# A mixture-of-experts stage whose 64-slot passes run beside 128-slot passes, chunk by chunk

## What is computed

```python
D_MODEL, D_FF, N_EXPERTS, TOP_K = 1024, 2816, 8, 2

def swiglu(h, w1, w3, w2):
    return (jax.nn.silu(h @ w1) * (h @ w3)) @ w2

def moe_ffn(h, router, w1, w3, w2):
    ht = h.reshape(-1, shape[-1])
    logits = (ht @ router).astype(jnp.float32)
    top_v, top_i = lax.top_k(logits, TOP_K)
    wts = jax.nn.softmax(top_v, axis=-1)
    combine = jnp.sum(jax.nn.one_hot(top_i, N_EXPERTS, dtype=jnp.float32) * wts[..., None], axis=1)
    # for every expert: out += combine[:, e] * swiglu(ht, w1[e], w3[e], w2[e])
```

## Time and profile before

| | before |
|---|---|
| median of three runs | 1789.32 us |
| lowest and highest of them | 1788.54 and 1793.39 us |
| the profiled execution | 1784.65 us |
| its span, first to last instruction | 1782.8 us |
| TensorE busy | 1676.5 us (94%) |
| VectorE busy | 1021.3 us (57%) |
| ScalarE busy | 792.6 us (44%) |
| read from HBM | 404.73 MB |

### The profile page before, as it was taken

The page is one execution under the profiler, slowest core; times in us unless marked ns, Lnnn a source line. Parts: engine busy times, 40 slices in busy tenths (PEclk is TensorE's granted clock), DMA queues, the critical chain, the costliest instruction groups (busy, mean ns, idle before and its releaser), DMA issues.

```text
span 1782.8 us, 25642 instructions
## 1 busy us (share of the span) xinstructions
PE 1676.5 (94%) x10193; PEld 1294.4 (73%) x10193; DVE 1021.3 (57%) x1415; ACT 792.6 (44%) x1225; POOL 55.0 (3%) x40
## 2 busy tenths in 40 slices
PE   5999987999999999999977999999999999988896
PEld 3877656988888888797767887677788888544443
DVE  3326656677677533733676987657889897100012
ACT  4417544532212222734655766556677776100101
POOL 0000000000000000000000530000000000000000
PEclk9999968999999999999988999999999999999998
DMA  8411053154467532131013986668989998999998
GB/s 335 161 62 72 1 188 144 72 189 174 157 228 262 197 116 95 57 142 63 33 50 142 352 331 227 247 230 328 361 341 356 345 368 313 378 406 421 419 420 363
DMA packets 56831, 407.53 MB, mean 229 GB/s; under 512 B 6322, under 2 KB 6450, under 8 KB 7808
## 3 DMA queue, kind: packets, MB, share of 16 engines
q1 hardware_dynamic: 56128, 404.38, 59.2%
q0 software_dynamic: 288, 0.79, 0.1%
q10 hardware_dynamic: 288, 0.63, 0.1%
HBM read 404.73 MB, written 1.05 MB: 228 GB/s over the span
## 4 chain that ended last, share of the span: by engine, by line
PE 82%; DMA 7%; DVE 6%; ACT 4%; issue 1%; SPq 0%; POOL 0%; ACTq 0%; DVEq 0%
PE psum L2273 60%; DMA raw<-units 5%; PE psum L2887 4%; PE psum L2897 2%; PE psum L2783 2%; DMA raw_more<-units 2%; PE psum L2841 1%; PE psum L2913 1%; PE psum L2925 1%; PE psum L2290 1%; PE psum L2472 1%; PE psum L2299 1%; DVE w_lo L1572 1%; PE psum L2496 1%; ACT xn L1026 1%
## 5 line engine op out<-in xcount | busy, mean ns | idle before, releaser
L1572 DVE TENSOR_TENSOR w_lo<-raw,w_hi 128x1024 fp32r<-128x1024 f32 x130 | 153.0, 1219 | 143.9 <-ACT w_hi L990 143.5
L2273 PE MATMUL psum<-act_hi,w_hi 128*128 128x512 f32 (+1 forms) x608 | 220.3, 362 | 2.8 <-DVE w_lo L1572 2.8
L2273 PE MATMUL psum<-act_hi,w_lo 128*128 128x512 f32 (+1 forms) x608 | 218.1, 359 | 0.0
L2273 PE MATMUL psum<-act_lo,w_hi 128*128 128x512 f32 (+1 forms) x608 | 218.0, 359 | 0.0
L990 ACT ACTIVATE w_hi<-raw 128x1024 fp32r<-128x1024 f32 x130 | 130.4, 1053 | 164.2 <-DMA raw<-units 89.8
L2044 DVE TENSOR_TENSOR w_lo<-raw,w_hi 128x2048 fp32r<-128x2048 f32 x75 | 171.4, 2289 | 45.4 <-ACT w_hi L1378 45.1
L1378 ACT ACTIVATE w_hi<-raw 128x2048 fp32r<-128x2048 f32 x75 | 143.8, 1918 | 73.0 <-PE psum L2273 43.8
L2273 PE MATMUL psum<-w_hi,act_hi 128*128 128x256 f32 (+1 forms) x368 | 131.2, 357 | 4.3 <-DVE act_lo L1651 2.4
L2044 DVE TENSOR_TENSOR w_lo<-raw_more,w_hi 128x2048 fp32r<-128x2048 f32 x49 | 112.1, 2289 | 35.7 <-ACT w_hi L1378 35.4
L2273 PE MATMUL psum<-w_hi,xt_hi 128*128 128x512 f32 x332 | 132.2, 398 | 0.0
L2093 DVE TENSOR_TENSOR e_act<-e_sil,psum 128x256 f32<-128x256 f32 (+1 forms) x88 | 32.2, 366 | 172.6 <-ACT e_sil L1452 172.6
(11 more groups left out here) (364 smaller groups left out, 3210.5 us busy)
## 6 DMA issues: line engine op xcount, KB each, us to landing
raw<-units SPq DMA_DIRECT2D x275, 1024.0 KB, 5.1
raw_more<-units SPq DMA_DIRECT2D x107, 1024.0 KB, 6.8
...
```

Source lines behind the costliest of these rows:

```text
L1572: ins = dve.tensor_tensor(w_lo[:, w_slot(i), part], raw[:, i % RING, part], w_hi[:, w_slot(i), part].bitcast(F32), ALU.subtract)
L2273: ins = pe.matmul(dst, lhs(a), rhs(b), start=first and n == 0, stop=last and n == 2)
```

## The change

The narrow passes are now p3, p5 and p7 (`NARROW`), and the experts that they take are the same three least used (`PLACE_OF_RANK`). Passes p2 and p3, p4 and p5, p6 and p7 run as pairs: `run_steps` yields rows, and a row of a pair holds one chunk of the full pass and one of the narrow. In such a row TensorE's order is: the full chunk's up (two units), the narrow chunk's up (two units), the turns of the row before, full and narrow, then the downs of the row before that, full and narrow. Each row so has six units. PSUM banks and several SBUF buffers are assigned anew, so that both passes have their own.

`splits_at` takes the place of `split_behind`. In p0 and p1 the splits run four units ahead as before, but only within these passes; in paired rows a unit is split in its own row, with none ahead. ScalarE and VectorE split the full up units first, copy the turns of the row before behind them, then take the SiLU or product of the full chunk, the split of the full down unit, and the SiLU or product of the narrow chunk.

The outputs of both passes of a pair are brought to SBUF in chunk 2 of the next pair, and their eight scatters stand in its chunks 2 to 9. The gathers are spread over chunks 7 to 10 as single pieces; those of p3 move into the wide pass, beside p2's. `finish` scatters, and VectorE adds, the output of both last passes, eight pieces instead of four. To bring the experts into the new places VectorE writes eight constants (`place_wanted`) in p0, and treats the narrow places one by one in `ranked` and `next_task`, which runs three times.

```diff
+PLACE_OF_RANK = (0, 1, 2, 5, 3, 6, 4, 7)
...
-def run_steps(passes):
-
-    g0, g1 = passes[0] * FC, (passes[-1] + 1) * FC
-    for g in range(g0, g1 + 2):
-        yield g if g < g1 else None, g - 1 if g0 <= g - 1 < g1 else None, g - 2 if g0 <= g - 2 else None
+NARROW, SLOTS = (3, 5, 7), 64
+FIRST_PAIR = 2
+
+def is_narrow(p):
+
+    return p in NARROW
+
+def run_steps(r):
+
+    rows = []
+    for p in RUNS[r]:
+        if not is_narrow(p):
+            beside = (p + 1,) if is_narrow(p + 1) else ()
+            rows += [tuple(q * FC + c for q in (p,) + beside) for c in range(FC)]
+    for i in range(len(rows) + 2):
+        yield tuple(rows[j] if 0 <= j < len(rows) else () for j in (i, i - 1, i - 2))
+
...
+SINGLE_SPLITS = sum(m < UNIT_AT["up", FIRST_PAIR * FC, 0] for m in SPLIT_LIST)
...
-def split_behind(r, key):
-
-    s = SPLIT_OF[UNIT_AT[key]] + W_RING
-    return [s] if s < split_limit(r) and s != LATE_SPLIT else []
-
-
-LATE_SPLIT = SPLIT_OF[UNIT_AT["down", NARROW[0] * FC - 1]]
+    return split_end(r) + (W_RING - 1 if r else 0)
+
+def splits_at(r, key):
+
+    s = SPLIT_OF[UNIT_AT[key]]
+    if r == 0 and s >= SINGLE_SPLITS:
+        return [s]
+    return [s + W_RING] if s + W_RING < (split_limit(r) if r else SINGLE_SPLITS) else []
+
+def last_passes(r):
+
+    return tuple(p for p in RUNS[r] if p > RUNS[r][-1] - 1 - is_narrow(RUNS[r][-1]))
+
+def scatters_at(r, p, c):
+
+    if r or p == 0 or is_narrow(p):
+        return []
+    if p == WIDE:
+        return [(0, c - SCATTER_STEP)] if SCATTER_STEP <= c < SCATTER_STEP + 4 else []
+    first = SCATTER_STEP - 1
+    out = [(p - 2 if p > FIRST_PAIR else WIDE, c - first)] if first <= c < first + 4 else []
+    return out + ([(p - 1, c - first - 4)] if first + 4 <= c < first + 8 and p > FIRST_PAIR else [])
+
...
+def outputs_at(r, p, c):
+
+    if r or c != 2 or p == 0 or is_narrow(p):
+        return []
+    return [p - 1] if p <= FIRST_PAIR else [p - 2, p - 1]
+
+def is_paired(r, i):
+
+    return r == 0 and i >= FIRST_PAIR * FC
+
...
+def gather_pieces(r, p, c):
+
+    if r or p == 0 or is_narrow(p) or not 0 <= c - GATHER_STEP < 4:
+        return []
+    a = p + 1 if p == WIDE else p + 2
+    pieces = [[(a, 0)], [(a, 1)], [(a, 2), (a + 1, 0)], [(a + 1, 1), (a + 1, 2)]][c - GATHER_STEP]
+    return [piece for piece in pieces if piece[0] <= EXPERTS]
 
 
...
         def run(r):
-            for up, turned, down in run_steps(RUNS[r]):
-                p, c = divmod(up, FC) if up is not None else (None, None)
-                if up is not None:
+            for i, (ups, turned, downs) in enumerate(run_steps(r)):
+                full = [g for g in ups if not is_narrow(g // FC)]
+                for g in full:
+                    p, c = divmod(g, FC)
                     if p == WIDE + 1 and c == 2:
                         wide_output()
-                    if not is_narrow(p):
-                        for s in split_behind(r, ("up", up, 0)):
+                    for s in splits_at(r, ("up", g, 0)):
+                        high(s)
+                    if p < FIRST_PAIR:
+                        for q in outputs_at(r, p, c):
+                            output(q)
+                    if p == WIDE:
+                        silu(g)
+                        wide_silu(g)
+                    for s in splits_at(r, ("up", g, 1)):
+                        high(s)
+                if is_paired(r, i):
+                    for g in full:
+                        for q in outputs_at(r, *divmod(g, FC)):
+                            output(q)
+                    for g in turned_into_rows(r, i):
+                        columns_turned(g)
+                    for q, piece in gathered_into_rows(r, i):
+                        half_high(q, piece) if piece < 2 else selection_turned(q)
+                for g in full:
+                    if g // FC != WIDE:
+                        silu(g)
+                if is_paired(r, i):
+                    for g in downs[:1]:
+                        for s in splits_at(r, ("down", g)):
                             high(s)
-                    if c == 2 and 0 < p < EXPERTS:
-                        output(p - 1)
-                    if p == WIDE:
-                        silu(up)
-                        wide_silu(up)
-                    if not is_narrow(p):
-                        for s in split_behind(r, ("up", up, 1)):
-                            high(s)
-                    if p != WIDE:
-                        silu(up)
-                if turned is not None:
-                    columns_turned(turned)
-                if down is not None and not is_narrow(down // FC):
-                    for s in split_behind(r, ("down", down)):
+                    for g in ups[1:]:
+                        silu(g)
+                    continue
+                for g in turned_into_rows(r, i):
+                    columns_turned(g)
+                for g in downs[:1]:
+                    for s in splits_at(r, ("down", g)):
                         high(s)
-                if up == NARROW[0] * FC:
-                    high(LATE_SPLIT)
-                if p == WIDE and c in (GATHER_STEP, GATHER_STEP + 1):
-                    half_high(p + 1, c - GATHER_STEP)
-                elif p == WIDE and c == GATHER_STEP + 2:
-                    selection_turned(p + 1)
-                elif c == GATHER_STEP and p + 1 < PASSES_OF:
-                    columns_high(p + 1)
-                if p == WIDE - 1 and c == GATHER_STEP + 1:
-                    wide_columns()
-                if p == WIDE - 1 and c == GATHER_STEP + 2:
-                    wide_selection_turned()
+                for q, piece in gathered_into_rows(r, i):
+                    half_high(q, piece) if piece < 2 else selection_turned(q)
+                for g in full:
+                    p, c = divmod(g, FC)
+                    if c == GATHER_STEP and (p == 0 or r and p + 1 < PASSES_OF):
+                        columns_high(p + 1)
+                    if p == WIDE - 1 and c == GATHER_STEP + 1:
+                        wide_columns()
+                    if p == WIDE - 1 and c == GATHER_STEP + 2:
+                        wide_selection_turned()
 
...
         def finish(p):
 
             act.activation(std[:, 0:1], eps, ACT.Sqrt).then_inc(sem("root_table"), 1)
-            output(p)
+            for q in last_passes(0) if p < EXPERTS else (p,):
+                output(q)
...
+            for q in last_passes(r):
+                output(q)
...
-            link(dve.tensor_tensor(order[:, :, :], by_row(place_of[:, :]), by_column(descending_once), ALU.is_equal))
+            for p, rank_of in enumerate(PLACE_OF_RANK):
+                link(dve.memset(place_wanted[:, p:p + 1], float(EXPERTS - rank_of)))
+            link(dve.tensor_tensor(order[:, :, :], by_row(place_of[:, :]), by_column(place_wanted[:, :]), ALU.is_equal))
...
-            link(dve.tensor_scalar(score[:, narrow], rank[:, narrow], float(SLOTS), None, ALU.is_gt))
+            for p in NARROW:
+                link(dve.tensor_scalar(score[:, p:p + 1], rank[:, p:p + 1], float(SLOTS), None, ALU.is_gt))
...
-            link(dve.tensor_reduce(top[:, 1:2], one[:, NARROW[0]:NARROW[-1] + 1], X_AXIS, ALU.add))
-            link(dve.scalar_tensor_tensor(place, top[:, 1:2].to_broadcast([P, 2]), float(P - SLOTS), place, ALU.mult, ALU.add))
+            for p in NARROW:
+                link(dve.scalar_tensor_tensor(place, one[:, p:p + 1].to_broadcast([P, 2]), float(P - SLOTS), place,
+                                              ALU.mult, ALU.add))
...
+            for q in last_passes(0)[:-1] if p < EXPERTS else ():
+                for n in range(4):
+                    added(q, n, n)
...
         def run(r):
-            for up, turned, down in run_steps(RUNS[r]):
-                if up is not None:
-                    up_chunk(up)
-                if turned is not None:
-                    turn_chunk(turned)
-                if down is not None:
-                    down_chunk(down)
-                if up is not None:
-                    p, c = divmod(up, FC)
-                    if p and p != RUNS[r][0] and SCATTER_STEP <= c < SCATTER_STEP + 4:
-                        scatter(p - 1, c - SCATTER_STEP, SCATTER_BANK)
-                    if p == WIDE and GATHER_STEP <= c < GATHER_STEP + 3:
-                        gather_in_wide(c - GATHER_STEP)
-                    elif c == GATHER_STEP and p + 1 < PASSES_OF:
+            for ups, turned, downs in run_steps(r):
+                for g in ups:
+                    up_chunk(g)
+                for g in turned:
+                    turn_chunk(g)
+                for g in downs:
+                    down_chunk(g)
+                for g in ups[:1]:
+                    p, c = divmod(g, FC)
+                    for q, n in scatters_at(r, p, c):
+                        scatter(q, n)
+                    for q, piece in gather_pieces(r, p, c):
+                        gather_piece(q, piece)
```

351 lines of the change are left out of this document (223 added, 128 removed).

## The result

The changed kernel takes 1818.37 us, the median of four runs (1816.33 to 1828.07), against 1789.68 us before: 1.0171 times as long, with a 95% interval of 1.0145 to 1.0196. I had forecast 1796 us and a range up to 1809. The direction is right, the size is not. In the profiled executions the span grew from 1782.8 to 1814.5 us, by 31.7.

A forecast was written before the change was run, and what follows sets the result against it. Full passes were bound by TensorE, narrow ones by loads. TensorE's -16, +4.8 ahead of p2 and +6 at the end net -5; loads add 12: +7, 1791.7 us profiled, 1796 as median, range 1783 to 1809.

The forecast's parts named there:

- TensorE's row at 14.0 us: Paired rows, p2's first chunk to the last down: TensorE needs 14.0 us for one full and one narrow chunk.
- The wait of 0.85 us behind the SiLU: Full down of each paired row: TensorE waits 0.85 us for the split queued behind the full SiLU, 33 times, 28 us.
- Gathers: Gathers of p4 to p7 in the paired rows: 3.8 us each for p4 and p6, 3.6 for p5 and p7, 14.8 together.
- Scatters: Scatters in the paired rows: 7.1 us for four of p1, 4.0 for eight full, 8.5 for eight narrow.
- p2's start: Start of p2: two last wide downs and, in its third row, a wait behind the wide output's copy, together 7.1 us.
- The loads, 2.67 us a unit, +12: Paired rows: loads come in bunches at 2.67 us a unit, 16.0 us a row, adding 12 us.
- My own sign of being wrong: Paired rows: the forecast is wrong if splits wait over 2 us per row for loads to land.
- loads run dry: Rival for the paired rows: 2.75 us a unit or more, as split, TensorE and next load wait in turn; 1808, chance 0.22.
- Up to p2: Ahead of p2: 3.8 us for p3's gather and turn in the wide pass, 1 for VectorE's small operations, +4.8 together.
- four units in advance cover most: p0: splits four units ahead hide most of VectorE's added 1.7 us of small operations, leaving 1.
- The end: Behind the last down: four more adds, 2.8 us, and a first add 3.1 us later through VectorE's branch; +6.
- HBM as a limit: Rival for the loads: HBM binds at about 358 GB/s, 17.6 us a row; 1841 us or so, chance 0.02.

The follow-up runs named there:

- e5: Changed kernel with six raw buffers, three split pairs, and the full down unit split ahead of the full SiLU: 1780.87 us, 0.9962 of the kernel before.
- e1: Changed kernel with six raw buffers instead of five and three pairs of split buffers instead of four: 1804.96 us, 1.0090 of the kernel before.
- e12: Changed kernel with the edits of e3, e4 and e7, last outputs behind the branch, and seven raw buffers, three split pairs from p2 on: 1759.79 us.
- e2: Changed kernel where from p2 on every load brings only the first half of its unit: 1796.77 us, 1.0046 of the kernel before.
- e3: Changed kernel with the full down unit split ahead of the full chunk's SiLU and product: 1809.34 us, 1.0115 of the kernel before.
- e4: Changed kernel with the wide output's copy behind both up splits in p2's third row: 1815.17 us, 1.0146 of the kernel before.
- e7: Changed kernel with VectorE's eight constants written ahead of p0 and its narrow places treated in one operation: 1818.45 us, profile only.
- e9: Changed kernel with three pairs of split buffers instead of four, the raw ring still five: 1823.35 us, profile only.

## Why the prediction was wrong, step by step

- **TensorE's row at 14.0 us:** too small. In e5, with hardly a load wait and none at the down, four of the five plain rows take 14.3 to 14.4 us. I had priced the fast blocks by the full passes, where like stands beside like. Beside plain float32 blocks the full up takes 5.57 us at least and not 5.44, and the full down 2.90 and not 2.83. Over the stretch, ups, turns, downs and the drain come to 509.7 us in e1 for my 496.5, 13.2 more. The two blocks make 4.3 and 2.5 of it. The clock at half in p2's third row, which I had at nothing, makes 2.5. The rest is spread, over full ups of 5.6 to 5.7 us and narrow downs of 1.87 among others.
- **The wait of 0.85 us behind the SiLU:** right, in mechanism and size: 0.84 by e1 and e5. Its place in the sum was right too: of my 28 us, e5 gives back 24.3, and e12, with loads in time, 27.6 (the turns' block, 11.0 for e1's 38.6).
- **Gathers:** one was left out. The pass that isn't run (p8) has its tokens gathered as well, in p6 and p7's rows. Ten pieces stand in the stretch and not eight, so 19.2 us and not 14.8. Scatters were right (19.6 for 19.6), and so were the narrow up at 3.6 and p2's start at 7.0.
- **The loads, 2.67 us a unit, +12:** this step failed. I looked for the nearest rate, but there was no rate to be found: the queues took what they were given, and they were given it late. The cause is the ring coming round late, by the two loops of the timeline above, and their terms all stood in the trace of before: the ring of five, six units to a row, 1.8 us for the narrow unit, 4.3 for the split, 5.7 to 10.6 for a load. I even wrote that four of a row's six units are held longer, and didn't follow one buffer round. It costs 19.8 us (e1, e2): 13.5 of TensorE standing still, 4.8 for three falls of the clock behind such waits, and small change. My own sign of being wrong was there: splits waited 82 us for landings, 2.5 us a row, where I had set 2. Of the rivals, "loads run dry" named the loop (the split waits for its load, TensorE for the split, the next load for TensorE), but its price of 2.75 a unit gave 1808: it priced the loads at 24 us, more than they cost, and left out TensorE's own 17.6.
- **Up to p2:** 7.8 for 4.8. The gather in the wide pass took its 3.7. The small operations took 1.7 and not the 1 I left of them, so "four units in advance cover most" was wrong: what VectorE adds there goes straight to TensorE. The clock's fall took 1.6, and 0.7 is from ahead of the expert passes.
- **The end:** 2.4 for 6. The read of the task and the branch cost 5.05 us behind VectorE's last output, near the 5.74 of the earlier trace rows. But that output isn't the last thing to wait for: behind the full down TensorE still does the narrow one, 1.94 us, and the output was through 0.1 us before that ended. I had put it 2.2 us behind it. And the 2.4 are partly luck. In six other kernels with the same end (e1, e3, e4, e5, e7, e9) the idle time is 5.3 to 6.9 us and the end 19.5 to 21.9, which is 2.8 to 5.2 over the 16.7 before; in e2 it is 16.8. Why it varies so is open. The Trainium skill, Advanced Engine Details and Errata, Control Flow Timing, gives a compare-and-branch about 0.1 us. The 5.05 us in the changed kernel's trace are for read and branch together, and no run parts the two.
- **HBM as a limit:** e12 moves 403 GB/s over 522 us. The 358 GB/s per core of the Trainium skill, DMA: Bandwidth & Descriptors, Where 436 GB/s comes from, do not bind here.

By the profiles the errors add up: 3.0 ahead of p2, 13.2 and 4.4 on TensorE, 7.8 for the loads beyond my 12, and -3.6 at the end, 24.8 in all. From the forecast's 1791.7 for the profiled execution that makes 1816.5; it took 1816.33.
